# Column strips for the first modulation and the gate rows of the first attention, and position-bias rows replicated DRAM to DRAM, in a three-layer float32 transformer kernel

## The reference

```python
cond = jax.nn.silu(c)
for layer in range(2):
    mod = cond @ w_ada[layer] + b_ada[layer]              # 1024 x 3072 weights
    shift, scale, gate = jnp.split(mod, 3, axis=-1)
    h = rmsnorm(x, g_pre[layer]) * (1.0 + scale) + shift
    y = mixer(h)                                           # two kinds of attention, silu gates, output projection
    x = x + gate * rmsnorm(y, g_post[layer])
```

## Time and profile before

| | us |
|---|---|
| three executions | 1510.01, 1509.82, 1513.34; median 1510.01 |
| the profiled execution | 1518.29 |
| its span, first to last instruction | 1516.2 |
| TensorE busy in it | 1280.7 (84%) |
| VectorE, ScalarE, GpSimd busy | 565.0, 426.0, 175.1 |
| mean granted clock of TensorE | 0.904 of 2.4 GHz |

### The profile page before, as it was taken

How to read it: one execution, slowest core, us unless ns; L and a number is a source line. 1 busy time by engine, 2 the same in 40 slices (tenths; PEclk the granted TensorE clock), 3 DMA queues, 4 the chain that set the end, 5 groups by cost and what they waited for, 6 DMA issues and landing times.

```text
span 1516.2 us, 14803 instructions
## 1 busy us (share of the span) xinstructions
PE 1280.7 (84%) x5128; PEld 727.6 (48%) x5128; DVE 565.0 (37%) x1408; ACT 426.0 (28%) x1078; POOL 175.1 (12%) x156
## 2 busy tenths in 40 slices
PE   1579989997997999899989989908999989966984
PEld 0455455664653444344456536604554455635541
DVE  4533323323235320334443232011223642566881
ACT  0133024543311101331245112102333443561211
POOL 0000003034410000000000000000000000275732
PEclk9989999977698999999999999958999899965987
DMA  9221321116323132321110212333111100100000
GB/s 313 97 83 29 99 96 56 56 56 240 130 47 85 27 56 56 70 60 56 48 46 1 68 42 45 82 77 140 42 42 42 42 28 29 56 1 29 1 29 28
DMA packets 60246, 99.68 MB, mean 66 GB/s; under 512 B 12063, under 2 KB 22124, under 8 KB 60173
## 3 DMA queue, kind: packets, MB, share of 16 engines
q1 hardware_dynamic: 54358, 93.56, 20.6%
q10 hardware_dynamic: 5814, 5.18, 1.1%
HBM read 94.64 MB, written 4.06 MB: 65 GB/s over the span
## 4 chain that ended last, share of the span: by engine, by line
PE 71%; DVE 13%; ACT 4%; another core or an unknown queue 4%; issue 3%; POOL 2%; ACTq 2%; DMA 1%; SPq 0%; DVEq 0%; POOLq 0%
PE PR L756 25%; PE SC L811 7%; PE PT L709 6%; PE OB L709 6%; PE OB L789 6%; PE SC L709 5%; PE PR L709 5%; PE PT L826 3%; PE PR L852 3%; DVE d L1529 2%; POOL arena L1429 2%; DVE stage L1521 2%; DVE d L1521 1%; PE PT L724 1%
## 5 line engine op out<-in xcount | busy, mean ns | idle before, releaser
L756 PE MATMUL PR<-ring,hT 128*128 128x512 f32 (+1 forms) x576 | 275.2, 590 | 36.1 <-DMA ring<-in_w_in 35.2
L789 PEld LDWEIGHTS OB<-arena,pts 128*128 128x128 f32 (+3 forms) x880 | 137.2, 208 | 112.0 <-issue 80.0
L1199 ACT ACTIVATE stage<-stage,nmax 128x256 f32<-128x256 f32 (+7 forms) x200 | 103.9, 520 | 299.8 <-DVE nmax L1777 280.9
L811 PE MATMUL SC<-arena 64*128 64x256 f32 (+15 forms) x432 | 154.1, 470 | 10.0 <-DVE nmax L1777 10.0
L756 PE MATMUL PR<-hT,ring 128*128 128x512 f32 (+1 forms) x304 | 156.5, 638 | 0.0
L756 PEld LDWEIGHTS PR<-ring,hT 128*128 128x128 f32 x576 | 99.8, 198 | 107.5 <-issue 63.0
L789 PE MATMUL OB<-arena,pts 128*128 128x64 f32 (+4 forms) x880 | 136.2, 286 | 16.6 <-ACT pts L1083 16.6
L1429 POOL TENSOR_TENSOR arena<-arena 128x192 f32<-128x192 f32 (+1 forms) x118 | 80.6, 683 | 515.6 <-PE OB L789 467.5
L826 PE MATMUL PT<-ident,stage 128*128 128x128 f32 (+3 forms) x440 | 90.7, 298 | 32.7 <-ACT stage L1178 14.5
L826 PEld LDWEIGHTS PT<-ident,stage 128*128 128x128 f32 (+3 forms) x440 | 58.8, 149 | 116.3 <-issue 52.3
L1083 ACT ACTIVATE pts<-PT 128x256 f32<-128x256 f32 (+7 forms) x200 | 80.9, 405 | 43.3 <-issue 24.6
(11 more groups left out here) (322 smaller groups left out, 1380.7 us busy)
## 6 DMA issues: line engine op xcount, KB each, us to landing
ring<-in_w_ada SPq DMA_DIRECT2D x12, 2048.0 KB, 9.5
ring<-in_od_w_in SPq DMA_DIRECT2D x8, 2048.0 KB, 14.2
ring<-in_w_in SPq DMA_DIRECT2D x5, 1536.0 KB, 6.8
ring<-in_ev_w_in SPq DMA_DIRECT2D x3, 2048.0 KB, 7.9
ring<-in_w_in SPq DMA_DIRECT2D x3, 2048.0 KB, 15.2
ring<-in_ev_w_out SPq DMA_DIRECT2D x2, 2048.0 KB, 7.9
ring<-in_od_w_out SPq DMA_DIRECT2D x2, 2048.0 KB, 8.2
ring<-in_w_out SPq DMA_DIRECT2D x2, 2048.0 KB, 8.5
```

Of the source, the lines that this page charges most:

```text
L756: mm = pe.matmul(dst, l, r, start=(k == 0), stop=(k == KT - 1))
L789: mm = pe.matmul(ob[:, h * w:h * w + w], pts[0:rows_, v % 2, n * P:n * P + P], vb, start=(n == 0), stop=(n == len(blocks) - 1))
L811: pe.matmul(SC[s % 2][:, 0:n], q, k, start=True, stop=True).then_inc(s_done, 1)
L1199: give(act.activation(pb[:, s % NP, 0:n], zm[:, s % 2, 0:n], ACT.Exp, bias=nmax[:, row, c:c + 1], scale=-1.0, accum_out=rsum[:, row, c:c + ...
```

## The change

Three things are changed.

1. **The start.** Layer 0's modulation is made on TensorE in column strips. A chunk's eight blocks are multiplied with a column of cond broadcast to 32 columns, so each result has 32 equal rows; block k goes to strip k mod 4 of one PSUM bank, and each strip adds up two blocks ("adas" tile). DVE copies the bank to d1 or d2, and the four matmuls per chunk use `pick`, a column with ones at partitions 0, 32, 64 and 96, in place of ones. DVE's order is written out anew, the first four transposes of x stand ahead of the fourth chunk, SP's first loads don't wait for the vector rows, and ACT computes the exponential for cond ahead of the constant loads.
2. **Gate rows in attention(0).** Each adag tile of eight matmuls becomes an adas tile (two units of four strip matmuls), a DVE copy to d3, and one matmul with `pick` broadcast (one unit), which first waits for that copy. The list and its spread are new: 28 units over the last 40 steps instead of 48.
3. **The bias rows.** The matmuls and copies move from the start of the second block to behind the "ckv" projection of layer 0. SP writes the six rows once to DRAM before chunk ("w", "gate0", 0), replicates them 128 times DRAM to DRAM before chunk ("ada", 0, 5), and reads them back skewed after issuing chunk ("w", "kvc"), once the last group of attention(1) is done.

```diff
-    + [(("ada", *chunk_), [(("adag", chunk_[0], chunk_[1] - 4) if chunk_[1] >= 4 else ("adac", *chunk_))])
-       for chunk_ in ((0, 4), (1, 0), (0, 5), (1, 1), (1, 4), (1, 2), (1, 5), (1, 3))],
+    + [(("ada", 0, 4), [("adas", 0, 4)]), (("ada", 1, 0), [("adac", 1, 0), ("adag", 0, 0)]),
+       (("ada", 0, 5), [("adas", 0, 5)]), (("ada", 1, 1), [("adac", 1, 1), ("adag", 0, 1)]),
+       (("ada", 1, 2), [("adac", 1, 2)]),
+       (("ada", 1, 4), [("adas", 1, 4)]), (("ada", 1, 3), [("adac", 1, 3), ("adag", 1, 0)]),
+       (("ada", 1, 5), [("adas", 1, 5), ("adag", 1, 1)])],
...
-SPREAD = [[(7, 24), (8, 40)], [(15, 15), (4, 31)], [(21, 68), (4, 14)]]
-UNITS = {"adac": 4}
+HT_FIRST = 4
+STRIPS = 4
+
+SPREAD = [[(7, 24), (12, 40)], [(15, 15), (4, 31)], [(21, 68), (4, 14)]]
+UNITS = {"adac": 4, "adas": 2, "adag": 1}
...
     for c in range(4):
-        chunk(("ada", 0, c), [("adac", 0, c)])
-    jobs.extend(("hT", 0, k) for k in range(KT))
+        if c == 3:
+            jobs.extend(("hT", 0, k) for k in range(HT_FIRST))
+        chunk(("ada", 0, c), [("adas", 0, c)])
+        jobs.append(("adac", 0, c))
+    jobs.extend(("hT", 0, k) for k in range(HT_FIRST, KT))
     chunk(("w", "cq"), [("cq", i) for i in range(T)])
     chunk(("w", "ckv"), [("ckv", i) for i in range(T)])
+    jobs.append(("relrow", 0))
+    jobs.append(("relrow", 1))
...
+        one = nc.dram_tensor("rel_row", [NSH, 640], F32, kind="Internal").ap()
         scr = nc.dram_tensor("rel_rows", [NSH, P, 640], F32, kind="Internal").ap()
...
-            sp.wait_ge(v_in, 16 * N_V)
             for n, c in enumerate(chunks):
...
+                    drained(sp, ("relrow", 1))
+                    sp.dma_start(one, relrow).then_inc(rel_out, 16)
+                if c == ("ada", 0, 5):
+                    sp.wait_ge(rel_out, 16)
+                    sp.dma_start(scr, bass.AP(one.tensor, one.offset, [[640, NSH], [0, P], [1, 640]])).then_inc(rep_out, 16)
...
-                if c == ("w", "cv1"):
-
-
-                    sp.wait_ge(relr_s, 1)
-                    sp.dma_start(scr, spread(relrow, P)).then_inc(rel_out, 16)
-                    sp.wait_ge(rel_out, 16)
+                if c == ("w", "kvc"):
+                    sp.wait_ge(rep_out, 16)
+                    sp.wait_ge(ob_free, g_no[1, len(plan[1]) - 1] + 1)
                     sp.dma_start(a2["B"], bass.AP(scr.tensor, scr.offset + P - 1,
                                                   [[639, P], [640 * P, NSH], [1, S]])).then_inc(rel_in, 16)
...
+                if kind == "adag":
+                    freed(pe, ("adas", name[1], name[2] + 4))
+                    pe.matmul(b[:, :], pick[:, :].to_broadcast([P, P]), d3[:, :], start=True,
+                              stop=True).then_inc(pr_done, 1)
+                    yield
+                    return
+                if kind == "adas":
+                    w = P // STRIPS
+                    for k in range(KT):
+                        j = k % STRIPS
+                        mm = pe.matmul(b[w * j:w * j + w, :], cond[:, k:k + 1].to_broadcast([P, w]), W[:, k, :],
+                                       start=(k < STRIPS), stop=(k >= KT - STRIPS))
+                        if k == KT - 1:
+                            mm.then_inc(pr_done, 1)
+                        if k % STRIPS == STRIPS - 1:
+                            yield
+                    return
...
             for c in range(4):
-                pe.wait_ge(acc_s, c + 1)
+                if c == 3:
+                    make_hT(0, upto=HT_FIRST)
+                W = weights(("ada", 0, c))
+                b = begin(("adas", 0, c))
+                w = P // STRIPS
+                for k in range(KT):
+                    j = k % STRIPS
+                    mm = pe.matmul(b[w * j:w * j + w, :], cond[:, k:k + 1].to_broadcast([P, w]), W[:, k, :],
+                                   start=(k < STRIPS), stop=(k >= KT - STRIPS))
+                mm.then_inc(pr_done, 1)
+                freed(pe, ("adas", 0, c))
                 b = begin(("adac", 0, c))
                 for m in range(4):
-                    mm = pe.matmul(b[:, m:m + 1], (d1, d2)[c % 2][:, m * P:m * P + P], ones[:, :],
+                    mm = pe.matmul(b[:, m:m + 1], (d1, d2)[c % 2][:, m * P:m * P + P], pick[:, :],
                                    start=True, stop=True)
                 mm.then_inc(pr_done, 1)
-            make_hT(0)
+            make_hT(0, first=HT_FIRST)
...
+            act.wait_ge(exp_b, 1)
+            say(act.activation(cond[:, :], cond[:, :], ACT.Exp, scale=-1.0), exp_c, "exp_c")
+            act.dma_start(onehot_r, C["onehot_r"]).then_inc(oh_in, 16)
+            act.dma_start(tbl[0:32, :], A["rel_bias_2"]).then_inc(oh_in, 16)
...
+                elif kind == "adas":
+                    b = take(dve, name)
+                    release(dve.tensor_copy(d3[:, :], b[:, :]), name)
...
-                    link(ts(t, W[:, 0, :], cond[:, 0:1], ALU.mult))
-                    for k in range(1, KT):
-                        ins = stt(t, W[:, k, :], cond[:, k:k + 1], t, ALU.mult, ALU.add)
...
+            link(dve.tensor_reduce(pick[:, :], ident[:, ::P // STRIPS], AX.X, ALU.add))
...
+            strip_sums(0)
+            dve.wait_ge(x_in, 16)
+            square_sum(0)
+            square_sum(1)
+            strip_sums(1)
+            modulation(0, 0)
+            square_sum(2)
+            square_sum(3)
+            strip_sums(2)
+            modulation(0, 1)
+            normalise(0)
+            modulation(0, 2)
+            strip_sums(3)
+            modulation(0, 3)
```

More of the change, by code:

```diff
@@ L335, in two_block_kernel @@
         ones = sb("ones", [P, 1])
+        pick = sb("pick", [P, 1])
         cond = sb("cond", [P, KT])
@@ L763, in whole_tile, with make_hT @@
                     pass
-            def make_hT(L):
+            def make_hT(L, upto=KT, first=0):
                 src = x if L == 2 else tok
-                for k in range(KT):
+                for k in range(first, upto):
                     if k == 0:
@@ L890, in _ @@
                 token_major(("ckv", i), W, i, 0, 288)
+            pe.wait_ge(oh_in, 32)
+            pe.wait_ge(pool_seq, 2)
+            for r in range(2):
+                b = begin(("relrow", r))
+                pe.matmul(b[0:NSH, 0:320], tbl, onehot_r[:, 320 * r:320 * r + 320],
+                          start=True, stop=True).then_inc(pr_done, 1)
             for i in range(T):
@@ L941, in _ @@
             pe.wait_ge(l2_in, 16 * N_L2)
-            pe.wait_ge(pool_seq, 4)
-            for r in range(2):
-                b = begin(("relrow", r))
-                pe.matmul(b[0:NSH, 0:320], a2["tbl"][:, 0:NSH], onehot_r[:, 320 * r:320 * r + 320],
-                          start=True, stop=True).then_inc(pr_done, 1)
             W = weights(("w", "kvc"))
@@ L1275, in _ @@
                           allow_slow_non_contiguous=True).then_inc(c_in, 16)
-            act.wait_ge(exp_b, 1)
-            say(act.activation(cond[:, :], cond[:, :], ACT.Exp, scale=-1.0), exp_c, "exp_c")
             rsqrt(T)
@@ L1879, in _ @@
                 release(tt(a0["krr"][:, i:i + 1, :], u, w, ALU.add), ("ckv", i))
+            for r in range(2):
+                b = take(dve, ("relrow", r))
+                release(dve.tensor_copy(relrow[:, 320 * r:320 * r + 320], b[0:NSH, 0:320]), ("relrow", r))
             for i in range(T):
@@ L1939, in _ @@
             hT_odd(2)
-            for r in range(2):
-                b = take(dve, ("relrow", r))
-                release(dve.tensor_copy(relrow[:, 320 * r:320 * r + 320], b[0:NSH, 0:320]), ("relrow", r))
             dve.wait_ge(l2_in, 16 * N_L2)
-            say(ts(rt[:, 0:1], rt[:, 0:1], 1.0, ALU.mult), relr_s, "relr_s")
             def blocks(n):
@@ L2109 @@
 N_C = 10
-N_L2 = 6
+N_L2 = 4
 def kernel(**inputs):
```

58 lines of the change are left out of this document (23 added, 35 removed).

## The result

The changed kernel took **1461.1 us** (median of 4, 1456.3 to 1462.5) beside 1509.9 us for the kernel before (1505.7 to 1513.3): a ratio of **0.967, interval 0.964 to 0.971**, so 48.8 us less. The forecast was 1456, its range 1436 to 1484.

The account below looks back on a forecast made before the run. TensorE (71% of the chain) bounds it, with waits at the bias-row write, the start and the first attention's loads. Bias rows 38.2, start 10.5 and gate rows 5 sum to 53.7 off 1510.0: 1456 us, range 1436 to 1484.

Parts of the forecast that it names:

- Bias rows removed: Before the third attention: TensorE's 35.2 us wait, 1.2 of bias matmuls and 1.8 of clock go, sum 38.2 us.
- Bias rows added: Matmuls behind ckv cost 1.2 us as now, small write and read-back nothing; the replication delays first-attention loads.
- R = 16.7: Replication time ahead of chunk (0, 5): 14.5 us on six engines at a load's rate plus 2.2 for landing.
- R + 5.8 + 5.8: First attention: replication, then two chunk loads in turn, so POOL starts chunk (1, 1) about 28 us after the replication's issue.
- the rival with R = 53.9: Replication as slow as the old write, 53.9 us; first attention from chunk (0, 5) on 37 us later, 1493; chance 0.12.
- the one that ends slower than before: Replication blocks SP's queue at chunk (0, 5) longer than everything gained, from 70 us; 90 us gives 1530; chance 0.03.
- Start: Kernel's start: strips replace DVE's sums, so cq begins at 53 instead of 63.5, 10.5 us gained, bounds 4 and 16.
- a chunk takes 4.0 us: At the start: strips overlap 1.7 times, a group of four takes 2.0 us, a chunk 4.0, bounds 1.7 and 6.9.
- better overlap or more engines: Replication takes 7.7 us, 8.5 us gained; strips run four at a time, 5 us at the start; about 1442; chance 0.20.
- Gate rows in the first attention: TensorE's work falls by 8 us, but the chain of loads decides, so 5 us gained; 17 at full clock, 13 lost at half.
- Wait stays: Second block: chunk nz or the bias tile still comes last elsewhere, so TensorE's wait remains; 1494; chance 0.02.
- no overlap: Strips run in turn, costing 6 us at the start and 10 in the attention; 1472; chance 0.08.

Follow-up runs that it names:

- The bias rows alone: Kernel before with only the new bias-row handling (early matmuls, small write, DRAM to DRAM replication, read-back): ratio 0.978, 33.0 us less.
- the start alone: Kernel before with only the changed start (strips, transposes between, no SP wait for vectors, earlier exponential): ratio 0.992, 12.4 us less.
- The gate rows alone: Kernel before with only the first attention's gate rows made by strips, no replication ahead of the loads: ratio 0.9955, 6.8 us less.
- Two edits that change the order and not the amount of work: Changed kernel with the replication moved to chunk dk and chunk (1, 3) loaded ahead of (1, 4): ratio 0.963, 1453.7 us.
- the repeated run: The changed kernel measured again without an edit: ratio 0.970 to the kernel before.
- The added matmuls: Changed kernel with twelve unused 504-column matmuls more in the first attention: ratio 0.975, 1473.1 us.

## Why the prediction was right, and where its terms were off

The sum was 53.7 us; 48.8 was measured. The places and the order of the terms were right, and the bias rows, the largest of them, were explained rightly. The closeness of the sum is partly luck: the start brought a little more than its term, the other two brought less, and two errors in the forecast of the replication nearly cancelled.

**Bias rows removed: 38.2 forecast, about 34 to 38 found.** Between the two profiles it is 38.1 (1.0 matmuls, 35.0 at the nz tile, 2.1 behind it). But the 35.0 is 33.1 to 36.0 if the other three executions with the old bias rows are taken, and the 2.1 shrinks to under 1 with them (217.2 to 217.9 us from the nz tile to the load of w_out, where the kernel before had 219.2 and the changed one 217.0). The bias rows alone gave 33.0. The wait was sized rightly; the forecast placed 1.8 us of clock in the nz tile itself, and that tile got no faster (7.50 us beside 6.95). A little of it came later: the steps of the third attention ran their first 384-column matmul pairs at 1.65 us before, and from 985.74 on at 0.91 now.

**Bias rows added: R = 16.7 forecast, a delay of 9.9 found.** While it ran alone the copy moved 154 GB/s; by an estimate from that rate its 1.97 MB take 12.8 us, and with 2 for landing about 15. When it landed isn't in the trace. The forecast added R in full ahead of the two loads: T0 + 28. POOL began (1, 1) at T0 + 26.35, which looks like a hit. But in the four kernels with the new filler list and no copy ahead POOL began it at T0 + 16.4 to 16.5, where the same sum without R gives 11.6. The load of (1, 1) is issued only at T0 + 8.3 (284.39 in the changed kernel), when its place in the ring is free, and lands 8.0 us after that without a copy ahead, 17.9 with it. So the step "R + 5.8 + 5.8" had the wrong parts: the data and the sum are ready to start at 16.4 by themselves, and the copy adds 9.9 to that, not 16.7.

The slow rate of the old write did belong to its source of six partitions: the same bytes in the same six pieces read from DRAM moved at 154 GB/s, where the old write had 25 at its end and 36 on average (1.97 MB in 53.9 us). So the rival with R = 53.9, and with it the one that ends slower than before, fell. The rule of the outermost dimension (the Trainium skill, DMA: Bandwidth & Descriptors, rules for kernel authors) agrees with both DMA views above: 3 tenths of the engines with 6, nearly all with 128. The matmuls behind ckv cost nothing visible: they lie at 85.05 to 86.3, and the transposes behind them still wait 2.51 us for the norm.

**Start: 10.5 forecast, 14.8 found at cq, about 12 where the attention begins.** The step that failed is "a chunk takes 4.0 us", from an overlap of 1.7 times. One group of four strips takes 0.99 us in the chain at full clock, where four 512-column matmuls in turn are 3.43: 3.5 times. So a chunk is 2.05 us. The first chunks took 3.64, where eight in turn at half clock would be 13.7; a group in the attention took 1.94 at a granted clock of 0.50 (TensorE's timeline, 306.48 us), so 3.64 fits half clock. The quarters of the earlier trace rows were no measure for strips of 512 columns. The Trainium skill (TensorE: Matmul & The Clock Gate, part 3 on packing) gives 2.38 times for three strips; for four this case shows more. Half of the rival "better overlap or more engines" was therefore the truth, at the start. But the forecast also took full clock for granted, and at half clock three of the four chunks came out near its 4.0 us. Of the 4 us between the forecast for cq (52.6) and 48.7, 1.5 came up to the end of normalising (36.15 instead of 37.6: the third chunk's strips ran from 27.13 in 3.25 us, not from 28 in 4.0), 1.7 in the transposes and the fourth chunk's strips (36.17 to 41.83, 5.7 us instead of 7.4), and 0.7 behind them. The forecast counted the whole gain at cq as gained; the start alone kept 12.4 of its 16.2 us up to T0, and 12.4 is also what it took off the time. So its term is nearer to 10.5 than the 14.8 makes it look.

**Gate rows in the first attention: 5 forecast, no gain found within this change.** The mechanism was named rightly: the chain of loads decides, not TensorE's work. It is worth looking at what a large cut became. TensorE's groups by line in the stage, first before (284 to 414 us), then after (270 to 400):

```profile
L756 PE MATMUL PR<-ring,cond 128*128 128x512 f32 x64 | 42.9, 759 | 3.8 <-DMA ring<-in_w_ada 3.8
L811 PE MATMUL SC<-arena 64*128 64x256 f32 (+2 forms) x78 | 34.9, 536 | 0.0
L789 PE MATMUL OB<-arena,pts 128*128 128x64 f32 x189 | 32.4, 307 | 6.9 <-ACT pts L1083 6.9
```

```profile
L844 PE MATMUL SC<-arena 64*128 64x256 f32 (+2 forms) x78 | 39.3, 596 | 0.0
L822 PE MATMUL OB<-arena,pts 128*128 128x64 f32 x194 | 37.5, 335 | 5.3 <-ACT pts L1128 5.3
L772 PE MATMUL PR<-ring,cond 128*32 128x512 f32 x64 | 12.0, 832 | 0.0
L756 PE MATMUL PR<-ones,arena 128*128 128x1 f32 x32 | 6.3, 267 | 11.9 <-POOL arena L1463 11.9
L764 PE MATMUL PR<-d,pick 128*128 128x512 f32 x8 | 5.9, 836 | 0.2 <-DVE d L1669 0.2
```

The filler matmuls went from 42.9 to 12.0 + 5.9 us, 25 less. Scores and values, the same work, went from 67.3 to 76.8 at the lower granted clock (0.57 beside 0.70). Groups overlap one another, so their times don't add up to the engine's. From T0 to dq TensorE's busy time fell only from 113.2 to 105.5 us, and its idle time rose from 10.7 to 17.4, with 11.9 of waits for POOL that weren't there before. That leaves the 1.0 of the table of events. Even that leans on the kernel before, the second longest of the five with the old list: with the replication ahead, the old list had 116.5 and 120.7, the new one 122.4 to 123.1. The gate rows alone, without a replication ahead, did take 6.8 us off the time. Two steps of the forecast failed. The second gate row was done at T0 + 62, not 55: TensorE ran much of this stretch at half clock and stopped 5.9 us for POOL, then 3.7 for probabilities held up by DVE. And so POOL came to (1, 3) at T0 + 80.4, not at 72 (the load and both row loads are issued right behind that gate row, at T0 + 62.2). The forecast of T0 + 88 for POOL's end became T0 + 96. Two edits that change the order and not the amount of work show that the chain of loads sets the length: they moved (1, 1) to T0 + 16.5 and (1, 3) to T0 + 49 and gave 8 to 11 us. That TensorE stops at T0 + 36 and goes on at T0 + 41.85 was forecast well (T0 + 35 and 44).

**What the rivals were worth.** "Wait stays" and "no overlap" are excluded by the rows above. That the clock alone holds the changed kernel's stage at its length is excluded by the repeated run: a higher clock, the same length within 0.3 us, more waiting. With the old list it is the other way round: no sum of POOL holds TensorE up for more than 2.1 us there, and the length goes with the clock.

**Still open.** Why the granted clock in the window attention is 0.55 to 0.64 with the new filler list and 0.70 to 0.78 with the old one is not settled. The added matmuls changed the list's TensorE work and not the clock's level. Why the second attention takes 294.4 us in one execution and 303.0 in another isn't settled either, and nor is where the strips' gain goes between cq and T0.

## What to carry to other kernels

Where a load is issued only after a computed row has left its buffer, look at what stands behind it in the queue: here the order of two chunks and the place of one copy were worth 8 to 11 us of the stage, while 25 us less of filler matmuls behind that copy gained nothing that could be measured. Before making work shorter, take one event that ends the stage and follow the chain back; if it is load, POOL, matmul, load, look first for an edit that moves the first of these. A broadcast write out of a few SBUF partitions was cheaper here as a small write and a copy within DRAM, early and beside other work. And profile a stage more than once before a few us of it are put down to an edit: the same stage with the same filler list took from 116.5 to 124.0 us.

## What the runs showed of the hardware that was not expected

- Four column strips of 32, float32, 512 columns: in the timeline 1.06 us a group at a granted clock of 1.00 and 1.94 at 0.50, where the same four matmuls in turn are 3.43 and 6.84 (4 x 1.71). Timeline of TensorE of the changed kernel:

```profile
283.27 1.06 PE L772 MATMUL PR<-ring,cond 128*32 128x512 f32 x8
...
306.48 1.94 PE L772 MATMUL PR<-ring,cond 128*32 128x512 f32 x8
```

- The granted clock of the first 30 us. The windows of the changed kernel, 5 to 35 and 375 to 399 us (TensorE, its loads, DVE, ACT and POOL busy; granted clock; DMA share; GB/s):

```profile
5.00:35.00 30.00, 15.67 (x73) 6.58 (x73) 11.21 (x27) 0.62 (x3) 0.00 (x0) 0.97 1.07 376
...
375.00:399.00 24.00, 23.84 (x99) 15.41 (x98) 7.88 (x25) 11.00 (x34) 0.00 (x0) 0.65 0.25 88
```

  The first line shows 0.97, yet the strips of that stretch take 3.64 us, against 2.05 at 39.78, and the small matmuls 1.87 against 1.05. There the durations fit half clock and the column doesn't show it.
- One DVE addition of 128 x 512 took 4.11 us while POOL was adding within the ring, and 4.12 in the repeated run; seven others of the same kind around the first attention took 0.69 to 1.00. Its neighbour took 0.69 beside the same POOL work; it reads PSUM, while the slow one reads SBUF alone. It held up the step behind it, and TensorE for 3.69 us. Timeline of DVE of the changed kernel:

```profile
325.15 0.69 DVE L1564 TENSOR_TENSOR d<-OB,fr 128x512 f32<-128x512 f32 x1
325.87 4.11 DVE L1564 TENSOR_TENSOR tok<-tok,d 128x512 f32<-128x512 f32 x1
```

- A copy from DRAM to DRAM with 6 outermost moved 154 GB/s, 26 an engine if six engines ran, where the write of the same bytes from six SBUF partitions had 7 an engine at its end.
